# Splitting three attentions into six pairs of heads between the halves of an output projection

## The chip, the cores and the metric

The kernel runs on one core of a Trainium2 chip. The metric is the device time of one launch in microseconds (us), as the median of several runs. Engines are called by the profile's names: PE (TensorE's matmuls), PEld (its weight loads), ACT (ScalarE), DVE (VectorE), POOL (GpSimd), SP (SyncE, which issues the weight transfers).

## What is computed

A sequence of 256 tokens of width 1024 goes through two blocks of two layers each, all in float32. The change lies in the mixer of the first block's second layer:

```python
c_q, c_kv, k_r, q_mem = split(h @ mla_w_in)        # 384, 256, 64, 512 columns
q  = (rmsnorm(c_q) @ w_uq).reshape(B, S, 8, 192)   # 128 plain + 64 rotary
kv = (rmsnorm(c_kv) @ w_ukv).reshape(B, S, 8, 256) # 128 keys + 128 values
q_nope, q_rope, k_nope = each head's part, rmsnorm over the head, rotary on q_rope
o = causal softmax attention, 8 heads, 256 queries, 256 keys
o_mem = softmax attention of q_mem's 4 heads into 256 memory tokens (no mask)
x = x + concatenate([o, o_mem]) @ w_out            # 1536 x 1024
```

Before and after the mixer stands a gated feed-forward layer (1024 to 2816 and back).

## The kernel before

**Weights** come in slots of 128 x 2048 float32 (1 MB). SP loads slot after slot in a fixed order into a ring of three buffers; ACT rounds each to a high part (`act_hi`, L233) and DVE takes the remainder (`dve_lo`, L238), so a product is three fast matmuls (`pe_weight`, L242 to L244: high x high, high x low, low x high). SP reloads a buffer once its remainder is taken (`lo_ready`); ACT overwrites a high part once PE has used the slot (`slot_used`). Products that use no weight slot (norm sums, scores, transposes, values) are plain float32 matmuls, which the profile counts as two instructions each.

**Order.** Each engine has its own program, written out by hand and executed in order; semaphores join them. The mixer of this layer is `pe_mla`, `act_mla`, `dve_mla` and `pool_mla` (L1331 to L1604). Its second half has two parts.

*The up-projection* makes seven products in PSUM, `chunk(0)` to `chunk(6)`: the rotary queries, heads 0 to 3 and 4 to 7 of keys and queries, and the values of the two token tiles (5 and 6). They take turns in banks 4 to 5 and 6 to 7. Chunks 0 to 4 are copied to SBUF by DVE (`copy(i)`), squared by POOL (`pool_mla`, L1522), summed over the head by PE (`sums(i)`, L340, two matmuls of 512 columns), turned into a factor by ACT (`factor(i)`: logarithm L326, exponential L330), and scaled by DVE (`norm(i)`, L879).

*The three attentions*, numbered 1 (the four memory heads), 2 and 3 (four causal heads each), use four banks at a time, 4 to 7 for attentions 1 and 3, 0 to 3 for 2. Each goes through the same chain: scores (PE, L789); mask for 2 and 3 (DVE, L819); row maximum and its negative (DVE, L823, L826); exponential with row sums (ACT, L835); reciprocal and scaling (DVE, L842, L846); transposes (PE, L800); copy to SBUF (ACT, L851); product with the values (PE, L808, L810); split of the result into high (ACT, L309) and low part (DVE, L313), which are the inputs of the output projection. The output projection (`pe_out`) accumulates in banks 0 to 3. It has six slots of two 128-row halves: slots 0 and 1 take the memory heads, 2 and 3 attention 2, 4 and 5 attention 3. Because attention 2 also occupies banks 0 to 3, the accumulator is cleared (`pe_clear_acc`, L303) after attention 2 is split. On PE the order is

```python
scores(1); scores(2); turn(1); attend(1); turn(2); scores(3); attend(2)
clear; out 0; out 1; out 2; turn(3); out 3; attend(3); out 4; out 5
```

Of the kernel before, what the change touches and what calls it, by code (L numbers as in the profile page):

```python
# [26 lines left out]
P = 128  # L27
# [82 lines left out]
def build(nc, d_slots, d_x, d_mem, d_params, d_params2, d_consts, d_lngb, d_out):  # L110
    with ExitStack() as ctx:
# [89 lines left out]
        att_act, att_dve, att_pe = ([sem(f"att_{e}{n}") for n in range(4)] for e in ("act", "dve", "pe"))  # L201
# [558 lines left out]
        ATT_MLA = (2, 3)  # L760
        ATT_SCALE = (128 ** -0.5, 128 ** -0.5, (128 + 64) ** -0.5, (128 + 64) ** -0.5)
        att_small = sb("att_small", [P, 4, 4, 8])

        def att_rows(n):

            return [att_small[:, n, i].rearrange("p (t h) -> p t h", t=2) for i in range(4)]
# [6 lines left out]
        def att_view(n, v):  # L773
            return v[:, 0:HEADS * (384 if n in ATT_MLA else 512)].rearrange("p (h k) -> p h k", h=HEADS)

        def att_ps(n, b):
            return ps[:, b:b + 4, 0:384 if n in ATT_MLA else 512]

# [4 lines left out]
        def pe_scores(pe, n, b, products):  # L783

            for h in range(HEADS):
                for t in range(2):
                    pairs = products(h, t)
                    for i, (q, k) in enumerate(pairs):
                        last = pe.matmul(att_tile(n, att_ps(n, b), t)[:, h], q, k[:, 0:att_keys(n, t)], start=(i == 0),  # L789
                                         stop=(i == len(pairs) - 1), skip_group_check=True)  # L790
            last.then_inc(att_pe[n], 1)

        def pe_turn(pe, n, b, probs):
            out, src = att_ps(n, b), att_view(n, probs)
            pe.wait_ge(att_dve[n], AD("probs"))
            for h in range(HEADS):
                for t in range(2):
                    for m in range(att_keys(n, t) // P):
                        o = m * 256 + (t - (n in ATT_MLA and m)) * P
                        last = pe.transpose(out[:, h, o:o + P], att_tile(n, src, t)[:, h, m * P:(m + 1) * P], ident)  # L800
            last.then_inc(att_pe[n], 1)

        def pe_attend(pe, n, b, probs_t, value):

            out, src = banks(b, 2, HEADS, T), att_view(n, probs_t)
            pe.wait_ge(att_act[n], AA("copied"))
            for h in range(HEADS):
                pe.matmul(out[:, h], value(h, 0), src[:, h, 0:T], start=True, stop=False, skip_group_check=True)  # L808
                o = out[:, h, P:T] if n in ATT_MLA else out[:, h]
                last = pe.matmul(o, value(h, 1), src[:, h, T:], start=False, stop=True, skip_group_check=True)  # L810
            last.then_inc(att_pe[n], 1)

        def dve_att_max(dve, n, b, probs):
# [3 lines left out]
            if n in ATT_MLA:  # L817

                dve.tensor_tensor(att_view(n, probs), src, bcast(const("causal"), HEADS), ALU.add).then_inc(att_masked, 1)  # L819
                src = att_view(n, probs)  # L820
                dve.wait_ge(att_masked, ATT_MLA.index(n) + 1)
# [6 lines left out]
        def act_att_exp(act, n, b, probs):  # L828
# [4 lines left out]
            for h in range(HEADS):  # L833
# [5 lines left out]
        def dve_att_scale(dve, n, probs):  # L839
# [4 lines left out]
            for t in range(2):  # L844
                v = att_tile(n, att_view(n, probs), t)
                last = dve.tensor_tensor(v, v, row_rec[:, t].unsqueeze(2).to_broadcast([P, HEADS, att_keys(n, t)]), ALU.mult)  # L846
# [6 lines left out]
        def act_att_parts(act, n, b, k0, at, m):  # L853

            act.wait_ge(att_pe[n], AP_("out"))
            act_split(act, banks(b, 2, HEADS, T)[:, k0:k0 + m], in_hi[:, at:at + m])

        def dve_att_parts(dve, sp, b, k0, at, m):
            dve_split(dve, sp, banks(b, 2, HEADS, T)[:, k0:k0 + m], in_hi[:, at:at + m], in_lo[:, at:at + m])


# [134 lines left out]
        SPLIT_GLA, SPLIT_LAT, SPLIT_MLA = 3, 11, 14  # L996
        SPLIT_B2, SPLITS2 = 17, 10
# [191 lines left out]
        def dve_gla(dve):  # L1189
# [98 lines left out]
            dve_att_parts(dve, SPLIT_MEMO[0], 4, 0, 8, 2)  # L1288
            dve_att_parts(dve, SPLIT_MEMO[0] + 1, 4, 2, 10, 2)
# [19 lines left out]
        m_probs = {1: view(9728, 2048), 2: view(11776, 2048), 3: view(9728, 2048)}  # L1309
        m_probs_t = view(13824, 2048)  # L1310
# [20 lines left out]
        def pe_mla(pe):  # L1331
# [75 lines left out]
            chunk(6)  # L1407

            pe.wait_ge(mla_act, MA("v1"))
            pe_scores(pe, 1, 4, lambda h, t: [(m_qm[:, h, t * P:(t + 1) * P], mem_k[:, h])])  # L1410

            def products(g):
                def of(h, t):
                    h = 4 * g + h
# [3 lines left out]
                return of  # L1418

            def value(g):  # L1420
                return lambda h, m: m_v[:, m, (4 * g + h) * P:(4 * g + h + 1) * P]
            pe.wait_ge(mla_dve, MD("qr_turned"))
            pe.wait_ge(rms_dve, RMS_CHUNK + 3)
            pe.wait_ge(rms_act, RA("log", RMS_CHUNK + 4))
            pe_scores(pe, 2, 0, products(0))
            pe_turn(pe, 1, 4, m_probs[1])
            pe_attend(pe, 1, 4, m_probs_t, lambda h, m: mem_v[:, m, h * P:(h + 1) * P])
            pe_turn(pe, 2, 0, m_probs[2])
            pe.wait_ge(split_lo, SPLIT_MEMO[1] + 1)
            pe.wait_ge(rms_dve, RMS_CHUNK + 5)  # L1430
            pe_scores(pe, 3, 4, products(1))
            pe_attend(pe, 2, 0, m_probs_t, value(0))
            pe.wait_ge(split_lo, SPLIT_MLA + 1)
            pe_clear_acc(pe)
            for i in range(3):
                pe_out(pe, L1_OUT, i, MLA_OUT_AT)
            pe_turn(pe, 3, 4, m_probs[3])
            pe_out(pe, L1_OUT, 3, MLA_OUT_AT)
            pe_attend(pe, 3, 4, m_probs_t, value(1))
            pe.wait_ge(split_lo, SPLIT_MLA + 2)  # L1440
            pe_out(pe, L1_OUT, 4, MLA_OUT_AT)
            pe.wait_ge(split_lo, SPLIT_MLA + 3)
            pe_out(pe, L1_OUT, 5, MLA_OUT_AT)

        def act_mla(act):
# [38 lines left out]
            def value(t):  # L1484
                wait_chunk(act, 5 + t)
                act.activation(m_v[:, t], chunk_ps(5 + t), ACT.Copy).then_inc(mla_act, 1)
            act_hi(act, c + 2)
            act_hi(act, c + 3)
            act_rms_factor(act, RMS_MEMQ[1], head_sums, m_qm_factor, 128)
            act_hi(act, c + 4)  # L1490
            factor(0)
            factor(1)
            act_hi(act, c + 5)
            factor(2)
            act_hi(act, c + 6)
            factor(3)
            value(0)
            factor(4)
            value(1)
            act_att_exp(act, 1, 4, m_probs[1])  # L1500
            act_hi(act, L1_OUT + 2)
            act_att_turned(act, 1, 4, m_probs_t)
            act_att_exp(act, 2, 0, m_probs[2])
            act_att_parts(act, 1, 4, 0, 8, 4)
            act_att_turned(act, 2, 0, m_probs_t)
            act_att_parts(act, 2, 0, 0, 0, 4)
            act_att_exp(act, 3, 4, m_probs[3])
            act_hi(act, L1_OUT + 3)
            act_hi(act, L1_OUT + 4)
            act_att_turned(act, 3, 4, m_probs_t)  # L1510
            act_hi(act, L1_OUT + 5)
            act_att_parts(act, 3, 4, 0, 4, 2)
            act_att_parts(act, 3, 4, 2, 6, 2)
            act_hi(act, L1_OUT + 6)
            act_hi(act, L1_OUT + 7)

        def pool_mla(pool):
            for i, (v, _, _) in enumerate(CHUNKS):
                pool.wait_ge(mla_dve, MD(f"copy{i}"))
                if i >= 2:  # L1520
                    pool.wait_ge(rms_pe, RMS_CHUNK + i - 1)
                pool.tensor_tensor(m_sq[i % 2], v, v, ALU.mult).then_inc(mla_sq, 1)  # L1522

        def dve_mla(dve):
# [26 lines left out]
            def norm(i):  # L1551
                dve_head_norm(dve, RMS_CHUNK + i, CHUNKS[i][0], CHUNKS[i][1], m_factor[i % 2])
            dve_lo(dve, c + 2)
            copy(0)
            dve_lo(dve, c + 3)
            dve_head_norm(dve, RMS_MEMQ[1], flat(m_qm), "memq1", m_qm_factor)
            copy(1)
            dve_lo(dve, c + 4)
# [4 lines left out]
            dve_lo(dve, c + 5)  # L1563
# [7 lines left out]
            dve_lo(dve, c + 6)  # L1571
            norm(3)
            norm(4)
            dve_att_max(dve, 1, 4, m_probs[1])
            dve_att_scale(dve, 1, m_probs[1])
            dve.wait_ge(rms_dve, RMS_CHUNK + 5)
            dve_att_max(dve, 2, 0, m_probs[2])
            dve_lo(dve, L1_OUT + 2)
            dve_att_scale(dve, 2, m_probs[2])
            dve_att_parts(dve, SPLIT_MEMO[1], 4, 0, 8, 4)  # L1580
            dve_att_max(dve, 3, 4, m_probs[3])
            dve_att_parts(dve, SPLIT_MLA, 0, 0, 0, 4)
            dve_att_scale(dve, 3, m_probs[3])
            dve_lo(dve, L1_OUT + 3)
            dve_lo(dve, L1_OUT + 4)
            dve_lo(dve, L1_OUT + 5)
            dve_att_parts(dve, SPLIT_MLA + 1, 4, 0, 4, 2)
            dve_att_parts(dve, SPLIT_MLA + 2, 4, 2, 6, 2)
            dve_lo(dve, L1_OUT + 6)
# [703 lines left out]
        def _(pool):  # L2293
# [9 lines left out]
            pool_mla(pool)  # L2303
# [235 lines left out]
```

## Time and profile before

| | us |
|---|---|
| median of 3 runs (2076.99 to 2081.15) | 2080.57 |
| time of the profiled execution | 2082.32 |
| span of the profiled execution | 2080.2 |
| PE busy in the span | 2047.2 |
| DVE, ACT, POOL busy in the span | 1271.8, 999.4, 86.8 |

The span runs from the first to the last instruction of the profile. PE's busy time is the time in which at least one matmul is in the array; it says nothing of how fast the array ran, which the granted clock tells (1.00 is full speed, 0.50 half).

### The profile page before, as it was taken

The numbers are of one execution on the slowest core, as the hardware profiler recorded it, in microseconds if no ns is written. First come the engines' busy times: TensorE is split into PE (matmuls) and PEld (weight loads), VectorE is DVE, ScalarE is ACT, GpSimd is POOL, SyncE is SP. The second block draws the span as 40 slices with busy tenths as digits, with TensorE's granted clock in tenths as the row PEclk, the third lists the DMA queues.
The fourth block names the chain that finished last, engine by engine and source line by source line (L and its number), as shares of the span: only waits on it lengthen the run. The fifth ranks groups of instructions, "written<-read, shape, count | busy, mean of one in ns | idle before, by whom it ended". The sixth has DMA issues, their size and how long they took to land.

```text
span 2080.2 us, 37327 instructions
## 1 busy us (share of the span) xinstructions
PE 2047.2 (98%) x15913; PEld 1959.2 (94%) x15928; DVE 1271.8 (61%) x1141; ACT 999.4 (48%) x929; POOL 86.8 (4%) x58
## 2 busy tenths in 40 slices
PE   9999999999999999899999999999999999999998
PEld 8999998999999998589999999999998999999997
DVE  6556655755665576637555665676446674676545
ACT  5545645543454356435344663544344554544333
POOL 2000000100000001101000000100000000100000
PEclk9999999999999999999999999999999999999999
DMA  7555453455555544125554434464554544464552
GB/s 297 182 181 182 166 178 118 161 188 181 181 203 182 192 179 174 61 87 206 181 187 179 164 141 163 176 243 166 183 192 157 197 142 142 167 228 183 192 181 102
DMA packets 51217, 362.31 MB, mean 174 GB/s; under 512 B 5680, under 2 KB 6832, under 8 KB 7728
## 3 DMA queue, kind: packets, MB, share of 16 engines
q1 hardware_dynamic: 49856, 353.05, 47.4%
q0 software_dynamic: 1264, 7.80, 1.1%
q8 instruction: 81, 1.33, 0.2%
q14 instruction: 16, 0.13, 0.0%
HBM read 359.78 MB, written 1.05 MB: 173 GB/s over the span
## 4 chain that ended last, share of the span: by engine, by line
PE 92%; DVE 3%; ACT 2%; DMA 1%; issue 1%; POOL 0%; DVEq 0%; SPq 0%; ACTq 0%; POOLq 0%
PE ps L242 22%; PE ps L243 22%; PE ps L244 22%; PE ps L518 3%; PE ps L519 3%; PE ps L517 3%; PE ps L289 2%; PE ps L290 2%; PE ps L291 2%; PE ps L501 1%; PE ps L495 1%; PE ps L496 1%; DMA raw<-in_slots 1%; PE ps L789 1%; PE ps L1619 1%
## 5 line engine op out<-in xcount | busy, mean ns | idle before, releaser
L238 DVE TENSOR_TENSOR wlo<-raw,whi 128x2048 fp32r<-128x2048 f32 x325 | 758.9, 2337 | 476.4 <-ACT whi L233 475.6
L242 PE MATMUL ps<-in_hi,whi 128*128 128x256 f32 x3596 | 1016.7, 283 | 3.8 <-DVE in_lo L313 3.5
L243 PE MATMUL ps<-in_lo,whi 128*128 128x256 f32 x3596 | 1006.5, 280 | 0.0
L244 PE MATMUL ps<-in_hi,wlo 128*128 128x256 f32 x3596 | 1005.3, 280 | 0.0
L233 ACT ACTIVATE whi<-raw 128x2048 fp32r<-128x2048 f32 x325 | 619.4, 1908 | 214.8 <-PE ps L244 184.4
L242 PEld LDWEIGHTS ps<-in_hi,whi 128*128 128x128 f32 x3596 | 678.6, 189 | 12.3 <-DVE in_lo L313 4.7
L243 PEld LDWEIGHTS ps<-in_lo,whi 128*128 128x128 f32 x3596 | 678.7, 189 | 3.5 <-issue 1.7
L244 PEld LDWEIGHTS ps<-in_hi,wlo 128*128 128x128 f32 x3596 | 678.4, 189 | 0.0
L242 PE MATMUL ps<-h_hi,whi 128*128 128x256 f32 x480 | 134.5, 280 | 0.0
L243 PE MATMUL ps<-h_lo,whi 128*128 128x256 f32 x480 | 133.9, 279 | 0.0
L244 PE MATMUL ps<-h_hi,wlo 128*128 128x256 f32 x480 | 133.9, 279 | 0.0
L642 ACT ACTIVATE h_hi<-ws 128x512 fp32r<-128x512 f32 x58 | 36.7, 633 | 196.0 <-PE ps L519 99.4
L712 DVE TENSOR_TENSOR h_lo<-ws,h_hi 128x512 fp32r<-128x512 f32 x58 | 40.9, 706 | 103.1 <-ACT h_hi L642 103.1
L636 ACT ACTIVATE ws<-ws 128x512 f32<-128x512 f32 x44 | 27.8, 632 | 148.1 <-DVE ws L695 148.1
L519 PE MATMUL ps<-whi,h_lo 128*128 128x512 f32 x240 | 94.9, 396 | 0.0
L518 PE MATMUL ps<-wlo,h_hi 128*128 128x512 f32 x240 | 94.9, 396 | 0.0
L517 PE MATMUL ps<-whi,h_hi 128*128 128x512 f32 x240 | 94.9, 395 | 0.0
L289 PE MATMUL ps<-whi,in_hi 128*128 128x256 f32 x320 | 91.1, 285 | 0.0
L242 PEld LDWEIGHTS ps<-h_hi,whi 128*128 128x128 f32 x480 | 90.2, 188 | 0.4
L243 PEld LDWEIGHTS ps<-h_lo,whi 128*128 128x128 f32 x480 | 90.2, 188 | 0.1
L244 PEld LDWEIGHTS ps<-h_hi,wlo 128*128 128x128 f32 x480 | 90.2, 188 | 0.0
L290 PE MATMUL ps<-wlo,in_hi 128*128 128x256 f32 x320 | 89.9, 281 | 0.0
(295 smaller groups left out, 2162.9 us busy)
## 6 DMA issues: line engine op xcount, KB each, us to landing
raw<-in_slots SPq DMA_DIRECT2D x333, 1024.0 KB, 4.8
ws<-in_lngb POOLq DMA_DIRECT2D x4, 1024.0 KB, 5.1
ws<-in_mem_t POOLq DMA_DIRECT2D x2, 1024.0 KB, 10.1
consts<-in_consts SPq DMA_DIRECT2D x1, 1600.0 KB, 14.6
consts<-in_consts POOLq DMA_DIRECT2D x1, 1472.0 KB, 6.7
x<-in_x_t SPq DMA_DIRECT2D x1, 1024.0 KB, 7.9
y<-x SPq DMA_DIRECT2D x1, 512.0 KB, 2.6
y<-x SPq DMA_DIRECT2D x2, 256.0 KB, 2.1
```

The lines of the kernel that those rows point to most:

```text
L233: act.activation(whi[:, j], raw[:, j], ACT.Copy).then_inc(hi_ready, 1)
L238: dve.tensor_tensor(wlo[:, j], raw[:, j], whi[:, j].bitcast(F32), ALU.subtract).then_inc(lo_ready, 1)
L242: pe.matmul(out, whi[:, j, o:o + n], hi, start=start, stop=False, skip_group_check=True)
L243: pe.matmul(out, whi[:, j, o:o + n], lo, start=False, stop=False, skip_group_check=True)
L244: return pe.matmul(out, wlo[:, j, o:o + n], hi, start=False, stop=stop, skip_group_check=True)
L289: pe.matmul(o, a_hi, w_hi, start=(k == 0), stop=False)
L290: pe.matmul(o, a_hi, w_lo, start=False, stop=False)
L291: last = pe.matmul(o, a_lo, w_hi, start=False, stop=(k == DT - 1))
L517: pe.matmul(o, hi[:, kk, a], whi[:, j, w], start=(first and kk == 0), stop=False, skip_group_check=True)
L518: pe.matmul(o, hi[:, kk, a], wlo[:, j, w], start=False, stop=False, skip_group_check=True)
L519: last = pe.matmul(o, lo[:, kk, a], whi[:, j, w], start=False, stop=False, skip_group_check=True)
L712: dve.tensor_tensor(flat(lo), src, flat(hi).bitcast(F32), ALU.subtract).then_inc(ffn_hl, 1)
```

## The change

The three attentions become six of two heads: 1 and 2 are the memory heads, 3 to 6 the causal heads. Each uses two banks, odd ones 6 and 7, even ones 4 and 5 (`pair_bank`), and its own pair of SBUF buffers by parity (`pair_probs`). The accumulator's banks 0 to 3 belong to the projection from then on; it is cleared right after `chunk(6)`. A slot of the projection is worked off in halves (`pe_out_part`: 24 matmuls for each 128-row half), and the halves stand between an attention's transposes, the next one's scores, and its product with the values. ACT and DVE get the same steps in an order that fits. The squares of chunks 0 to 4 move from POOL to ACT (`square`); `pool_mla` is gone. DVE's remainders of four weight slots come one or two steps later. The number and the shapes of PE's matmuls and transposes stay the same. The core of the diff (the helpers take `ATT_HEADS[n]` in place of `HEADS` throughout):

```diff
-        ATT_MLA = (2, 3)
+        ATT_MLA = (3, 4, 5, 6)
+        ATT_HEADS = (HEADS, 2, 2, 2, 2, 2, 2)
+        def pe_out_part(pe, c, i, at, kk, ms):
+            j = (c + i) % RING
+            if kk == 0:
+                pe.wait_ge(lo_ready, c + i + 1)
+            a_hi, a_lo = in_hi[:, at[2 * i + kk]], in_lo[:, at[2 * i + kk]]
+            for m in ms:
+                last = pe_weight(pe, acc[:, m], j, kk * D + m * P, a_hi, a_lo, False, False)
+            return last
...
+        PAIR_AT = (8, 10, 0, 2, 4, 6)
+        def pair_bank(n):
+            return 6 if n % 2 else 4
+        def pair_probs(n):
+            return m_probs[(n - 1) % 2], m_probs_t[(n - 1) % 2]
...
+            def scores(n):
+                if n >= 3:
+                    pe.wait_ge(split_lo, SPLIT_MEMO[1] + n - 2)
...
+            def out(i, kk, ms=range(DT)):
+                if kk == 0:
+                    pe.wait_ge(split_lo, SPLIT_MEMO[1] + i + 1)
+                return pe_out_part(pe, L1_OUT, i, MLA_OUT_AT, kk, ms)
+            pe.wait_ge(mla_act, MA("v0"))
+            scores(1)
+            chunk(6)
+            pe.wait_ge(rms_act, RA("log", RMS_CHUNK + 4))
+            pe_clear_acc(pe)
+            pe.wait_ge(mla_act, MA("v1"))
+            scores(2)
+            turn(1)
+            attend(1)
             pe.wait_ge(mla_dve, MD("qr_turned"))
             pe.wait_ge(rms_dve, RMS_CHUNK + 3)
...
+            scores(3)
+            out(0, 0)
+            turn(2)
+            out(0, 1, range(4))
+            attend(2)
+            out(0, 1, range(4, DT)).then_inc(slot_used, 1)
+            for n in range(3, 7):
+                turn(n)
+                if n == 4:
+                    pe.wait_ge(rms_dve, RMS_CHUNK + 5)
+                if n < 6:
+                    scores(n + 1)
+                out(n - 2, 0)
+                attend(n)
+                out(n - 2, 1).then_inc(slot_used, 1)
+            out(5, 0)
+            out(5, 1).then_inc(slot_used, 1)
...
         def act_mla(act):
...
+            def square(i):
+                act.wait_ge(mla_dve, MD(f"copy{i}"))
+                if i >= 2:
+                    act.wait_ge(rms_pe, RMS_CHUNK + i - 1)
+                act.activation(m_sq[i % 2], CHUNKS[i][0], ACT.Square).then_inc(mla_sq, 1)
...
             act_hi(act, c + 2)
+            act_rms_factor(act, RMS_MEMQ[1], head_sums, m_qm_factor, 128)
+            square(0)
             act_hi(act, c + 3)
+            square(1)
+            factor(0)
             act_hi(act, c + 4)
             factor(1)
+            square(2)
+            square(3)
+            factor(2)
             act_hi(act, c + 5)
+            square(4)
             factor(3)
             value(0)
             factor(4)
+            exp(1)
             value(1)
+            act_hi(act, L1_OUT + 1)
+            turned(1)
+            parts(1)
+            exp(2)
             act_hi(act, L1_OUT + 2)
+            exp(3)
+            turned(2)
+            parts(2)
+            for n in range(3, 7):
+                turned(n)
+                if n < 6:
+                    exp(n + 1)
+                parts(n)
+                act_hi(act, L1_OUT + n)
             act_hi(act, L1_OUT + 7)
...
         def dve_mla(dve):
...
             norm(3)
+            att_max(1)
             norm(4)
+            scale(1)
+            att_max(2)
+            dve_lo(dve, L1_OUT + 1)
+            parts(1)
+            att_max(3)
+            scale(2)
+            dve_lo(dve, L1_OUT + 2)
+            scale(3)
+            parts(2)
+            for n in range(3, 7):
+                if n < 6:
+                    att_max(n + 1)
+                parts(n)
+                if n < 6:
+                    scale(n + 1)
+                dve_lo(dve, L1_OUT + n)
             dve_lo(dve, L1_OUT + 7)
...
-            pool_mla(pool)
```

## Rows read from the trace of the kernel before

**Rows 1.** The page: span and busy time of each engine.
```profile
span 2080.2 us, 37327 instructions
...
PE 2047.2 (98%) x15913; PEld 1959.2 (94%) x15928; DVE 1271.8 (61%) x1141; ACT 999.4 (48%) x929; POOL 86.8 (4%) x58
```

**Rows 2.** Busy time by stage, all engines.
```profile
core 0: us, PE busy (x) PEld busy (x) DVE busy (x) ACT busy (x) POOL busy (x), PEclk, DMA share, GB/s
...
600.00:780.00 180.00, 180.00 (x1539) 179.83 (x1538) 110.65 (x96) 81.08 (x66) 3.89 (x3) 1.00 0.51 185
780.00:936.00 156.00, 139.91 (x897) 117.74 (x897) 86.51 (x69) 76.32 (x104) 13.64 (x6) 0.97 0.30 108
```

**Rows 3.** TensorE's waits, 740 to 980 us: total, times, longest.
```profile
PE ps L340 <- POOL ws L1522: 5.0, 2, 3.0
PE ps L800 <- DVE ws L846: 2.8, 2, 1.9
PE ps L303 <- DVE in_lo L313: 2.6, 1, 2.6
PE ps L808 <- ACT ws L851: 2.0, 1, 2.0
PE ps L242 <- DVE in_lo L313: 1.9, 2, 1.4
PE ps L789 <- ACT ws L1486: 1.1, 1, 1.1
```

**Rows 4.** Clock in stretches of 4 us of that stage (columns as Rows 2).
```profile
828.00:832.00 4.00, 4.00 (x20) 3.38 (x19) 1.29 (x2) 2.17 (x2) 1.89 (x1) 0.60 0.26 107
848.00:852.00 4.00, 3.80 (x6) 1.71 (x7) 1.23 (x1) 0.02 (x1) 0.15 (x1) 0.57 0.56 233
...
868.00:872.00 4.00, 3.42 (x16) 3.15 (x16) 3.97 (x4) 0.00 (x0) 0.00 (x0) 0.60 0.00 0
...
892.00:896.00 4.00, 1.40 (x10) 1.05 (x11) 2.43 (x3) 3.75 (x14) 0.00 (x0) 1.00 0.00 0
```

**Rows 5.** The chain that ended last in the stage: start us, us, what.
```profile
855.79 3.74 PE ps L789 x16
...
868.59 3.57 PE ps L800 x16
...
874.05 3.51 ACT ws L835 x16
...
881.23 8.16 PE ps L789 x32
...
934.88 0.43 DVE x L748
```

**Rows 6.** ScalarE in order of time.
```profile
809.79 1.05 ACT L322 ACTIVATE ws<-ws 128x1024 f32<-128x1024 f32 x1
```

**Rows 7.** Weight loads in order of time, start of the stage.
```profile
809.68 0.19 PEld L242 LDWEIGHTS ps<-in_hi,whi 128*128 128x128 f32 x1 [0.91 <-DVE in_lo L313]
...
813.88 0.30 PEld L340 LDWEIGHTS ps<-ws,consts 128*128 128x128 f32 x2
```

**Rows 8.** Groups by shape, 811 to 935 us.
```profile
L1522 POOL TENSOR_TENSOR ws<-ws 128x1024 f32<-128x1024 f32 x5 | 13.4, 2685 | 74.8 <-DVE ws L1549 74.8
...
L819 DVE TENSOR_TENSOR ws<-ps,consts 128x1536 f32<-128x1536 f32 x2 | 3.5, 1754 | 8.6 <-PE ps L789 8.6
...
L851 ACT ACTIVATE ws<-ps 128x1536 f32<-128x1536 f32 x2 | 2.9, 1452 | 7.3 <-PE ps L800 7.3
...
L846 DVE TENSOR_TENSOR ws<-ws,att_small 128x512 f32<-128x512 f32 x2 | 1.4, 692 | 0.1
L823 DVE TENSOR_REDUCE att_small<-ws 128x4 f32<-128x512 f32 x2 | 1.4, 686 | 0.1
L313 DVE TENSOR_TENSOR in_lo<-ps,in_hi 128x512 fp32r<-128x512 f32 x2 | 1.3, 686 | 3.3 <-ACT in_hi L309 3.3
...
L309 ACT ACTIVATE in_hi<-ps 128x512 fp32r<-128x512 f32 x2 | 1.1, 594 | 5.0 <-PE ps L810 5.0
```

More of the change, by code:

```diff
@@ L200, in build @@
         gla_act, gla_dve, gla_pe, gla_norm = sem("gla_act"), sem("gla_dve"), sem("gla_pe"), sem("gla_norm")
-        att_act, att_dve, att_pe = ([sem(f"att_{e}{n}") for n in range(4)] for e in ("act", "dve", "pe"))
+        att_act, att_dve, att_pe = ([sem(f"att_{e}{n}") for n in range(7)] for e in ("act", "dve", "pe"))
         att_masked, mla_sq = sem("att_masked"), sem("mla_sq")
@@ L759, in build @@
         AP_, AD, AA = steps("scores", "turned", "out"), steps("max", "neg", "recip", "probs"), steps("exp", "copied")
-        ATT_MLA = (2, 3)
-        ATT_SCALE = (128 ** -0.5, 128 ** -0.5, (128 + 64) ** -0.5, (128 + 64) ** -0.5)
-        att_small = sb("att_small", [P, 4, 4, 8])
+        ATT_MLA = (3, 4, 5, 6)
+        ATT_SCALE = (128 ** -0.5,) * 3 + ((128 + 64) ** -0.5,) * 4
+        ATT_HEADS = (HEADS, 2, 2, 2, 2, 2, 2)
+        att_small = sb("att_small", [P, 7, 4, 8])
         def att_rows(n):
-            return [att_small[:, n, i].rearrange("p (t h) -> p t h", t=2) for i in range(4)]
+            return [att_small[:, n, i, 0:2 * ATT_HEADS[n]].rearrange("p (t h) -> p t h", t=2) for i in range(4)]
         def att_keys(n, t):
@@ L783, in pe_scores @@
         def pe_scores(pe, n, b, products):
-            for h in range(HEADS):
+            for h in range(ATT_HEADS[n]):
                 for t in range(2):
@@ L795, in pe_turn @@
             pe.wait_ge(att_dve[n], AD("probs"))
-            for h in range(HEADS):
+            for h in range(ATT_HEADS[n]):
                 for t in range(2):
@@ L803, in pe_attend @@
         def pe_attend(pe, n, b, probs_t, value):
-            out, src = banks(b, 2, HEADS, T), att_view(n, probs_t)
+            out, src = banks(b, ATT_HEADS[n] // 2, ATT_HEADS[n], T), att_view(n, probs_t)
             pe.wait_ge(att_act[n], AA("copied"))
-            for h in range(HEADS):
+            for h in range(ATT_HEADS[n]):
                 pe.matmul(out[:, h], value(h, 0), src[:, h, 0:T], start=True, stop=False, skip_group_check=True)
@@ L817, in dve_att_max @@
             if n in ATT_MLA:
-                dve.tensor_tensor(att_view(n, probs), src, bcast(const("causal"), HEADS), ALU.add).then_inc(att_masked, 1)
+                dve.tensor_tensor(att_view(n, probs), src, bcast(const("causal"), ATT_HEADS[n]), ALU.add).then_inc(att_masked, 1)
                 src = att_view(n, probs)
@@ L832, in act_att_exp @@
             act.wait_ge(att_dve[n], AD("neg"))
-            for h in range(HEADS):
+            for h in range(ATT_HEADS[n]):
                 for t in range(2):
@@ L845, in dve_att_scale @@
                 v = att_tile(n, att_view(n, probs), t)
-                last = dve.tensor_tensor(v, v, row_rec[:, t].unsqueeze(2).to_broadcast([P, HEADS, att_keys(n, t)]), ALU.mult)
+                last = dve.tensor_tensor(v, v, row_rec[:, t].unsqueeze(2).to_broadcast([P, ATT_HEADS[n], att_keys(n, t)]), ALU.mult)
             last.then_inc(att_dve[n], 1)
@@ L1406, in pe_mla @@
             sums(4)
[L1407 to L1412, printed above, removed]
+            def scores(n):
+                if n >= 3:
+                    pe.wait_ge(split_lo, SPLIT_MEMO[1] + n - 2)
                 def of(h, t):
-                    h = 4 * g + h
+                    if n < 3:
+                        h = 2 * (n - 1) + h
+                        return [(m_qm[:, h, t * P:(t + 1) * P], mem_k[:, h])]
+                    h = 2 * (n - 3) + h
                     r = slice(64 * (h % 2), 64 * (h % 2) + 64)
@@ L1417, in of, with turn, attend, value @@
                             (m_qr[r, h // 2, t * P:(t + 1) * P], m_kr[r, :])]
-                return of
-            def value(g):
-                return lambda h, m: m_v[:, m, (4 * g + h) * P:(4 * g + h + 1) * P]
+                pe_scores(pe, n, pair_bank(n), of)
+            def turn(n):
+                pe_turn(pe, n, pair_bank(n), pair_probs(n)[0])
+            def attend(n):
+                def value(h, m):
+                    if n < 3:
+                        h = 2 * (n - 1) + h
+                        return mem_v[:, m, h * P:(h + 1) * P]
+                    h = 2 * (n - 3) + h
+                    return m_v[:, m, h * P:(h + 1) * P]
+                pe_attend(pe, n, pair_bank(n), pair_probs(n)[1], value)
@@ L1423, in pe_mla @@
             pe.wait_ge(rms_dve, RMS_CHUNK + 3)
[L1424 to L1443, printed above, removed]
+            scores(3)
@@ L1486, in value, with exp, turned, parts @@
                 act.activation(m_v[:, t], chunk_ps(5 + t), ACT.Copy).then_inc(mla_act, 1)
+            def square(i):
[3 more added lines that the diff above has]
+                act.activation(m_sq[i % 2], CHUNKS[i][0], ACT.Square).then_inc(mla_sq, 1)
+            def exp(n):
+                act_att_exp(act, n, pair_bank(n), pair_probs(n)[0])
+            def turned(n):
+                act_att_turned(act, n, pair_bank(n), pair_probs(n)[1])
+            def parts(n):
+                act_att_parts(act, n, pair_bank(n), 0, PAIR_AT[n - 1], 2)
             act_hi(act, c + 2)
+            act_rms_factor(act, RMS_MEMQ[1], head_sums, m_qm_factor, 128)
+            square(0)
             act_hi(act, c + 3)
-            act_rms_factor(act, RMS_MEMQ[1], head_sums, m_qm_factor, 128)
+            square(1)
+            factor(0)
             act_hi(act, c + 4)
-            factor(0)
             factor(1)
+            square(2)
+            square(3)
+            factor(2)
             act_hi(act, c + 5)
-            factor(2)
-            act_hi(act, c + 6)
+            square(4)
             factor(3)
@@ L1552, in norm, with att_max, scale, parts @@
                 dve_head_norm(dve, RMS_CHUNK + i, CHUNKS[i][0], CHUNKS[i][1], m_factor[i % 2])
+            def att_max(n):
+                dve_att_max(dve, n, pair_bank(n), pair_probs(n)[0])
+            def scale(n):
+                dve_att_scale(dve, n, pair_probs(n)[0])
+            def parts(n):
+                dve_att_parts(dve, n, SPLIT_MEMO[1] + n - 1, pair_bank(n), 0, PAIR_AT[n - 1], 2)
             dve_lo(dve, c + 2)
             copy(0)
-            dve_lo(dve, c + 3)
             dve_head_norm(dve, RMS_MEMQ[1], flat(m_qm), "memq1", m_qm_factor)
             copy(1)
-            dve_lo(dve, c + 4)
+            dve_lo(dve, c + 3)
             norm(0)
@@ L1562, in dve_mla @@
             copy(3)
-            dve_lo(dve, c + 5)
+            dve_lo(dve, c + 4)
             dve.wait_ge(mla_turn, MT("qr"))
```

58 lines of the change are left out of this document (11 added, 47 removed).

## Prediction

> **What bounds the kernel now.** I read the page first: PE is busy for 2047.2 of 2080.2 us and no other engine for more than 61% [rows 1], so only time in which PE waits, or runs at a lower clock, can be won. Next, busy time by stage. In a feed-forward stage PE is busy for 180.00 of 180 us; in the stage that holds the changed mixer for 139.91 of 156 us, at a mean clock of 0.97 [rows 2]. That is where the kernel has slack, and the change touches nothing else. The part it rewrites begins with the first matmul of `chunk(0)` at 809.7 us [rows 7] and ends when DVE adds the finished projection to x at 934.9 us [rows 5]: 125.2 us. The waits of PE name what it loses there: 5.0 us for POOL's squares, 2.8 for scaled probabilities (L846) before transposes, 2.6 and 1.9 for low parts of an attention's result, 2.0 for the copy of transposed probabilities, 1.1 for the value copy; 15.4 us together [rows 3]. About 0.5 of it is the wait just ahead of `chunk(0)` (the weight load there was free for 0.91 us) [rows 7], so I count 14.9 us of waiting in the part. Then the clock: it was at the lower of its levels, 1.2 in place of 2.4 GHz, for most of three stretches of 4 us, with means of 0.60, 0.57 and 0.60 [rows 4]. Each costs 4 x 0.4 or so, 1.65 us, and the three 4.9. What is left, 125.2 - 14.9 - 4.9 = 105.4 us, is PE's work at full speed.
>
> **What the change leaves alone.** PE's matmuls stay: same number, same shapes, only their order differs, so 105.4 us stay. PE gets more waits, some two dozen, but a wait whose event is long past shows no gap in the trace, so I charge nothing; a tenth of a microsecond each would be 2.4, which goes into the range. SP's order of slots is the same. Four remainders (slots 3 and 4 of the up-projection, 0 and 1 of the output) come behind one more DVE step of 1.3 us or an attention step; each is still done 5 us or more before PE needs it, by the walk below, and the loads that wait for them start as much later, with as much to spare. Slots 2 to 5 of the projection are prepared once a round, a whole round ahead.
>
> **Squares.** A square costs 2.7 us on POOL on average (13.4 for five) [rows 8], on ACT 1.05 (the same size, L322) [rows 6]. That takes 1.65 us out of copy, square, sum. The 5.0 us of PE's waits for POOL came to 2.0 and 3.0; the second (square 4) goes altogether, since `copy(4)` also comes earlier, with no clock loss ahead of it, and PE has `chunk(5)` to do. ACT executes in order, so square 2 stands behind `factor(1)`, which waits for `sums(1)`, and square 3 for `copy(3)`. Walking the three queues forward with these durations I get one wait of 0.6 us, for square 2 ahead of `sums(2)`. The five squares add 5.2 us to ACT, which was busy for 76.3 of 156 us [rows 2]; its waits cover them.
>
> **Attentions 1 and 2 (memory).** Halved steps cost: transposed copy (L851, 1.45 for four causal heads) 0.8, with memory's wider tile 1.0; exponential (3.51 for four heads [rows 5]) 1.85 with the last row sum; mask 0.9 from 1.75; reductions 1.3 (2 x 0.69, causal 1.1); scaling 1.4 (causal 1.1); split 0.6 and 0.69 [rows 8]; scores of a memory pair 1.9 and a causal pair 4.1 from 3.74 and 8.16 [rows 5]. The walk from there:
> - scores(1) needs only the first value copy and runs before `chunk(6)`, so the 1.1 us wait goes. But ACT does exp(1) before the second value copy, and exp(1) waits for maximum and negative. `chunk(6)` (12 matmuls of 512 columns at twice 0.117, 2.8 us) and the clear (four of 512, 0.9) don't quite cover it: scores(2) waits 1.0.
> - turn(1) finds its probabilities ready. attend(1) waits for the copy with nothing placed between: 1.2 (2.0 before).
> - scores(3) takes banks 6 and 7 over from attention 1, so it waits until both parts of attention 1 are split: 0.6 + 0.69 and hand-overs. New, 1.6.
> - Half a slot (24 matmuls at 0.117, since 36 took 4.2 us [rows 7], 2.8 us) then covers part of DVE's mask, maxima, negative and scale(2), which stand in this order behind scores(3): turn(2) waits 1.2.
> - attend(2) is covered by the quarter slot ahead of it.
>
> **The rounds.** From n = 3 on a round is turn, scores(n+1), half slot, attend, half slot: 0.65 + 4.1 + 2.8 + 1.4 + 2.8 = 11.75 us of PE. (The transposes: 3.57 us for 16 instructions at the lower clock [rows 5] makes 0.67 for six at the higher; the product with the values: four instructions of 256 columns at 0.23, from scores(1), and four of 128 at half of it.) Behind scores(n+1) mask, maxima, negative and exponential take 0.9 + 1.1 + 0.2 + 1.85 = 4.05, against half slot and attend, 4.2. Behind attend come high part 0.6, low part 0.69, reciprocal 0.2 and scaling 1.1, 2.7 with overlaps, against the last half slot's 2.8. So PE doesn't wait, by a hair. The splits that cost 2.6 and 1.4 of waiting before [rows 3] now have a half slot behind them, the last one too.
>
> **Sum.** New waits 0.6 + 1.0 + 1.2 + 1.6 + 1.2 = 5.6 for 14.9: 9.3 us less. The clock: before, its falls stood behind waits for POOL (2.0 and 3.0) and behind the 0.9 ahead of turn(1), yet a wait of 2.6 us at 892 left it at 1.00 [rows 3, 4]; the trace gives no fixed length from which it falls. No new wait is above 1.6, but four stand within 20 us. Bounds: no fall (4.9 gained) to three (nothing); I take one, near the row at 868, so 4.9 - 1.65 = 3.25 gained. That makes 12.5; I round to 13, since POOL no longer runs beside DVE in this part. By the profiled execution the span would be 2067.2. Its own time, 2082.32, is 1.75 above the median, so I take the difference off the median: 2080.57 - 13 = 2067.5.
>
> The clock is also where a page speaks against the change. The Trainium skill, "TensorE: Matmul & The Clock Gate", section "A second HAM failure mode: psum-queue depth-cycling", says that a PE which idles briefly again and again between groups of matmuls while it cycles through PSUM banks sees its clock go down and up. By that rule the lower clock would come in most rounds, as in the third case below; the trace agrees only for the stretch at 868, not for 892.
>
> **Rivals.** Bounds first: without any fall and with two waits fewer the gain is 14.9 - 4 + 4.9 = 16 us (2064.5).
> 1. *The forecast*, 2064 to 2070: 0.60.
> 2. *The handoffs become the bound.* The margins of the rounds are 0.1 us. For it speaks that DVE and ACT run parts, scaling and slot work in one queue; against it that both are busy for under 60% of the part [rows 2]. One microsecond late in each of four rounds, or ACT late with each square (5 x 1), gives 4 to 5 back: 2072, range 2070 to 2074. 0.17.
> 3. *The clock falls three to five times* through the short steps, 3.3 to 6.6 us more than forecast: 2071 to 2074. For it, the fall behind a wait of 0.9; against it, that each round has 5.6 us of the dense matmuls that ran at 1.00 throughout. 0.10.
> 4. *Nothing comes of it*: the first feed-forward slots are late, so the gain is given back at the next stage. They are prepared behind attention 6 and wait for slots 3 and 4 to be used; I see their remainders done 1 us before the projection ends. 2077 to 2084: 0.05.
> 5. *Slower*: the clock stays at 1.2 GHz through the rounds. From 850 us on PE has about 65 us of work at full speed, and each microsecond of it at the half clock costs one more; from 12.5 us so spent the gain is gone. With two rounds at the half clock (23 us) the time is 2091. Turn(1) took 3.57 us for 16 instructions at the lower clock [rows 5], so it does reach transposes; but before no low stretch lasted beyond 4 us [rows 4]. 0.08.
>
> **How the numbers follow.** The likeliest case gives 2067.5, by itself 2064 to 2070. The runs of one kernel differ by up to 4 us, so its lower end becomes 2062, and cases 2 and 3 take the range to 2075; that leaves out cases 4 and 5 and the tails. A change of 0.2% (4.2 us) is about what a measurement of this kernel can tell. Faster: 0.60 + 0.17 + 0.10 = 0.87; same 0.06; slower 0.07; case 4 falls within 0.2%, case 5 all but one in eight on the slow side.
>
> **What would show it.** POOL has nothing between the mix squares and the end of the mixer. No wait of PE for L340's input above 1 us. Scores(3) waits 1.6 us for L313. From the third round of the projection on PE's busy time is full, and the part takes about 112 us. Wrong would be: waits of PE for DVE L846 in each round, PE's clock below 0.8 in several stretches after 850 us, or a wait of PE for a weight slot (L238) at the start of the next feed-forward.

## The result and the profile after

The changed kernel takes 2066.9 us (median of four runs, 2065.5 to 2068.5) where the kernel before, on the same chip, takes 2080.9 (2077.0 to 2081.4). The ratio is 0.9938, 95% interval 0.9923 to 0.9952, so it is faster by 14.0 us or 0.6%. The forecast was 2067.5.

TensorE's waits in the window of [rows 3]:

```profile
PE ps L790 <- DVE in_lo L313: 1.5, 1, 1.5
PE ps L809 <- ACT ws L852: 1.1, 1, 1.1
PE ps L790 <- ACT ws L1526: 0.8, 1, 0.8
PE ps L273 <- ACT in_hi L603: 0.6, 1, 0.6
PE ps L242 <- DVE in_lo L313: 0.5, 1, 0.5
PE ps L340 <- ACT ws L1531: 0.4, 1, 0.4
```

L790, L809 and L340 are scores, product with the values, and norm sums. Without the 0.6 and 0.5 us, which lie outside the part, PE waits 3.8 us for 14.9 before: 0.4 ahead of `sums(2)`, 0.8 ahead of scores(2), 1.1 ahead of attend(1), 1.5 ahead of scores(3). Those are the waits of the walk (0.6, 1.0, 1.2, 1.6), each a tenth or two shorter; the fifth, 1.2 ahead of turn(2), is missing. The next view, busy time in stretches, tells why (columns as in [rows 2], the clock is the third value from the end):

```profile
852.00:856.00 4.00, 2.60 (x14) 1.80 (x12) 3.42 (x4) 1.27 (x2) 0.00 (x0) 1.00 0.00 0
856.00:860.00 4.00, 2.78 (x11) 1.69 (x11) 0.69 (x1) 3.97 (x10) 0.00 (x0) 0.93 0.74 262
860.00:864.00 4.00, 4.00 (x11) 2.48 (x12) 0.96 (x2) 0.00 (x0) 0.00 (x0) 0.50 0.00 0
864.00:868.00 4.00, 4.00 (x28) 4.00 (x28) 3.93 (x7) 1.86 (x8) 0.00 (x0) 0.72 0.00 0
868.00:872.00 4.00, 4.00 (x30) 3.79 (x29) 1.93 (x4) 1.49 (x2) 0.00 (x0) 1.00 0.46 152
```

The clock fell right after the three waits, once, and stayed at 1.2 GHz for some 7 us (4 x (0.07 + 0.50 + 0.28) = 3.4 us lost, at half speed 6.8 us long). The chain shows what it cost (start us, us, what):

```profile
855.75 0.61 ACT in_hi L309
856.38 0.70 DVE in_lo L313
...
857.22 5.75 PE ps L790 x16
...
867.49 0.87 PE ps L801 x8
...
872.90 0.65 PE ps L801 x6
873.55 3.98 PE ps L790 x16
...
884.66 0.66 PE ps L801 x6
885.31 3.98 PE ps L790 x16
...
896.41 0.66 PE ps L801 x6
...
908.16 0.66 PE ps L801 x6
...
921.37 0.44 DVE x L748
```

Scores(3) took 5.75 us, scores(4) and (5), the same work, 3.98. The half slot behind scores(3) ran slowly too, long enough for DVE to have turn(2)'s probabilities ready at 867.49. So part of what the lower clock cost was time that PE would otherwise have waited. From 872.90 on the rounds start every 11.75 us (872.90, 884.66, 896.41, 908.16) with no wait, the length that the forecast added up. POOL has no instruction in the part, as forecast. The part begins at 809.5 us and ends at 921.4, 111.8 us long (125.2 before, about 112 forecast).

The span fell by 16.5 us, 3.1 more than the part. The remainder, from the end of the part to the end of the span, is the same program: 1145.3 us before, 1142.3 after. Over all the profiles of this study it lies between 1140.5 and 1145.3, with low-clock stretches near 1220 and 1700 us of the execution now longer, now shorter. They explain the spread. Adding up length times one minus clock over all stretches of 4 us of the remainder gives 8.2 us lost before and 4.4 after, and what is left of the remainder without its loss is between 1136.9 and 1137.9 us in each of the 13 profiles. So the 3 us that the span fell beyond the part are clock, not work.

The same split can be made for every execution, since each has its span and mean clock on record. Span times clock, an estimate of the time at full clock throughout (good to 1 us, because the clock is given to three decimals), has a median of 2064.7 us over 34 executions of the kernel before (2062.5 to 2066.2) and of 2053.4 over 14 of the changed one (2052.0 to 2054.6). About 11 us of the gain are waits and order, and the 3 to 5 that are left are a clock that is low for less time, in the part and behind it.

### The profile page after: what moved, and what is told of

Read it like the earlier page. It is cut to its first block, busy times and chain, and to the rows that moved or that the text cites. A ratio compares the mean times of both kernels' runs of the same rounds, so it can differ in the third digit from the quotient of the medians.

```text
span 2063.7 us, 37372 instructions
## 1 busy us (share of the span) xinstructions
PE 2042.7 (99%) x15928; PEld 1956.7 (95%) x15928; DVE 1267.6 (61%) x1163; ACT 1004.7 (49%) x939; POOL 73.3 (4%) x53
## 4 chain that ended last, share of the span: by engine, by line
PE 94%; DVE 3%; ACT 2%; DMA 1%; issue 1%; DVEq 0%; SPq 0%; ACTq 0%
PE ps L242 23%; PE ps L244 22%; PE ps L243 22%; PE ps L518 3%; PE ps L519 3%; PE ps L517 3%; PE ps L291 2%; PE ps L289 2%; PE ps L290 2%; PE ps L790 1%; PE ps L501 1%; PE ps L495 1%; PE ps L496 1%; DMA raw<-in_slots 1%; ACT whi L233 1%; PE ps L340 1%
## 5 line engine op out<-in xcount | busy, mean ns | idle before, releaser
L238 DVE TENSOR_TENSOR wlo<-raw,whi 128x2048 fp32r<-128x2048 f32 x325 | 755.6, 2327 | 456.5 <-ACT whi L233 455.7
```

Of the source, the lines that this page charges most:

```text
L238: dve.tensor_tensor(wlo[:, j], raw[:, j], whi[:, j].bitcast(F32), ALU.subtract).then_inc(lo_ready, 1)
```

## The experiments

All comparisons are with runs of the kernel before on the same chip. "Part" is the stretch from the first matmul of `chunk(0)` to the first addition to x, in the profiled execution. Rows with the same time before ran on the same chip.

| kernel | median us (runs) | before | ratio, 95% interval | part us |
|---|---|---|---|---|
| changed | 2066.9 (4) | 2080.9 | 0.9938, 0.9923 to 0.9952 | 111.8 |
| squares alone | 2074.3 (9) | 2080.3 | 0.9973, 0.9964 to 0.9983 | 117.0 |
| split alone | 2067.6 (5) | 2080.3 | 0.9942, 0.9929 to 0.9956 | 114.4 |
| filled waits | 2064.4 (5) | 2080.3 | 0.9920, 0.9907 to 0.9934 | 109.8 |
| no interleaving | 2099.4 (4) | 2080.3 | 1.0090, 1.0074 to 1.0105 | 146.8 |
| changed, second | 2065.4 (5) | 2079.6 | 0.9931, 0.9917 to 0.9945 | 111.8 |
| slot work first | 2071.3 (5) | 2079.6 | 0.9960, 0.9946 to 0.9973 | 117.8 |
| no interleaving, filled | 2085.3 (7) | 2079.6 | 1.0027, 1.0016 to 1.0038 | 131.9 |
| filled and shifted | 2064.6 (5) | 2079.6 | 0.9918, 0.9903 to 0.9933 | 109.4 |
| changed, third | 2063.6 (5) | 2079.4 | 0.9927, 0.9913 to 0.9941 | 113.4 |
| split alone, second | 2066.6 (5) | 2079.4 | 0.9942, 0.9928 to 0.9955 | 114.4 |
| filled and shifted, second | 2064.6 (5) | 2079.4 | 0.9927, 0.9913 to 0.9940 | 109.3 |

### The squares alone

```diff
 # kernel before, act_mla
             act_rms_factor(act, RMS_MEMQ[1], head_sums, m_qm_factor, 128)
+            square(0)
             act_hi(act, c + 4)
+            square(1)
             factor(0)
             factor(1)
+            square(2)
+            square(3)
             act_hi(act, c + 5)
             factor(2)
             act_hi(act, c + 6)
+            square(4)
             factor(3)
...
-            pool_mla(pool)
```

> The kernel before with one part of the change: the five squares on ACT instead of POOL, three attentions and the projection as before. Theory A (the squares matter through TensorE's clock and the DVE instructions that POOL stretched): the 5.0 us of waits for POOL shrink to about 3, since walking the queues forward with the rows' durations leaves PE's waits at 13.5 us for 14.2, but the two low-clock stretches behind the POOL waits (828 and 848 us) go and DVE's remainders next to a square fall from 3.3 to 4.0 us back to 2.3: 3 to 5 us faster, near 2077. Rival B (only the length of the waits counts): under 1 us, no measurable change, and the low-clock stretches stay.

6.0 us faster, a little more than the 3 to 5 of theory A. TensorE's waits, and DVE's remainders (L238: shortest, median and longest ns) in this kernel and in the one before:

```profile
PE ps L800 <- DVE ws L846: 2.8, 2, 1.9
PE ps L303 <- DVE in_lo L313: 2.6, 1, 2.6
...
PE ps L340 <- ACT ws L1491: 1.5, 2, 1.0
```

```profile
L238 DVE TENSOR_TENSOR wlo<-raw,whi x5: 2279/2293/2293, 811.5 to 840.8; 128x2048 fp32r<-128x2048 f32 x5
```

```profile
L238 DVE TENSOR_TENSOR wlo<-raw,whi x5: 2276/2293/4033, 812.7 to 844.1; 128x2048 fp32r<-128x2048 f32 x5
```

The squares now cost 1.5 us of waiting for 5.0, where the walk had left 3; the waits of the attentions are as before. The longest remainder fell from 4.03 to 2.29 us, so the slow ones were those beside POOL. In the profiled execution the clock stayed at 1.00 through the whole part and the part was 8.2 us shorter: 3.5 of waits, the rest the low clock. The fall at 868 us is gone too, though the wait of 0.9 ahead of turn(1) is still there, so that wait alone doesn't make it. This profile is of the fastest of nine executions, which spread from 2069 to 2079 us, wider than any other kernel here. The spread goes with the clock: the fastest has a mean clock of 0.998 and the two slowest 0.992, and 0.006 of the span is 12 us. Which stretches it fell in is known for the profiled one only.

### The split alone

```diff
 # changed kernel
-            square(0)            # and 1 to 4, in act_mla
...
+            pool_mla(pool)       # as before
```

> The changed kernel with the squares back on POOL. Theory A: walking forward, PE's waits in the part grow from 5.5 to 7.9 us, and one or two low-clock stretches of 1.7 us come back with the waits for POOL: 3 to 6 us slower than the changed kernel, 2070 to 2073. If the two parts of the change are independent, its gain and that of the squares alone add up to the 14 us of the whole. Rival B: the squares are hidden, 2067 to 2068.

> The changed kernel with the squares on POOL, on the same chip as the changed kernel. The medians so far, from two chips, lie 0.7 us apart, but in the profiled executions the part took 4 us longer with POOL. Theory A (the squares bring something only where PE's waits ahead of the sums are not made up for later; the 3.1 us of waits for POOL are on PE's path): 3 to 4 us slower than the changed kernel. Rival B (what POOL costs is given back, since a low-clock stretch falls there instead of at scores(3)): within 1 us.

12.8 us faster than before both times. The first time, 2067.6 us lies in the range of rival B and below that of theory A, but the changed kernel had run on another chip. Beside the changed kernel on the same chip it is 3.0 us slower (2066.6 and 2063.6, the ranges of the runs don't meet: 2066.3 to 2067.7 and 2063.5 to 2065.7), at the lower end of theory A. The profile of the second time:

```profile
PE ps L340 <- POOL ws L1575: 3.1, 2, 2.4
PE ps L790 <- DVE in_lo L313: 1.5, 1, 1.5
...
PE ps L801 <- DVE ws L847: 0.7, 1, 0.7
```

```profile
840.00:844.00 4.00, 1.62 (x5) 0.67 (x4) 4.00 (x2) 1.16 (x2) 2.94 (x1) 0.88 0.35 104
844.00:848.00 4.00, 4.00 (x11) 2.29 (x10) 0.02 (x1) 1.20 (x2) 0.00 (x0) 0.69 0.37 158
...
860.00:864.00 4.00, 3.66 (x15) 2.21 (x16) 0.19 (x1) 3.09 (x7) 0.00 (x0) 1.00 0.61 246
```

The wait for POOL is 3.1 us in all, the low clock comes behind it (844) and not at scores(3) (860), and the wait of 0.7 for DVE at turn(2) is back. The first profile shows the same, with the low clock from 846 to 850. The three waits ahead of scores(2), attend(1) and scores(3) are 0.8, 1.1 and 1.5 us as in the changed kernel, and yet the clock is 1.00 behind them in both profiles. So the two parts don't add up: 6.0 and 12.8 us alone, 14.0 to 15.8 together. Rival B's mechanism is seen, but it gives back only a part.

### No half slots between the steps

```diff
 # changed kernel, pe_mla (act_hi and dve_lo of slots 3 to 7 follow the last attention too)
             scores(3)
-            out(0, 0)
             turn(2)
-            out(0, 1, range(4))
             attend(2)
...
                 turn(n)
                 scores(n + 1)
-                out(n - 2, 0)
                 attend(n)
-                out(n - 2, 1).then_inc(slot_used, 1)
+            for i in range(6):
+                out(i, 0)
+                out(i, 1).then_inc(slot_used, 1)
```

> The changed kernel with pairs of heads, their banks and the squares on ACT, but with no half slot between the steps: all six slots of the projection follow the last attention, and their weight preparation follows it too. Theory A (the half slots are what hides the chains): walking forward, PE's waits grow from 5.5 to 28 us, and low-clock stretches with them, 2 to 5 of them at 1.7 us: 26 to 31 us slower than the changed kernel, 2093 to 2098, so slower than before. Rival B (finer attentions alone bring the gain, by overlapping with one another): within 5 us of the changed kernel, 2067 to 2072.

19 us slower than before and 32.5 slower than the changed kernel, which had run on another chip (33.0 when each is taken against the kernel before on its own chip). That is a little beyond theory A's 26 to 31. Waits, and the clock in four of the stretches:

```profile
PE ps L801 <- DVE ws L847: 16.2, 4, 5.0
PE ps L809 <- ACT ws L852: 3.1, 3, 1.1
PE ps L790 <- DVE in_lo L313: 2.3, 2, 1.5
```

```profile
884.00:888.00 4.00, 2.09 (x9) 1.87 (x10) 1.80 (x4) 0.52 (x1) 0.00 (x0) 0.50 0.02 4
888.00:892.00 4.00, 4.00 (x10) 2.25 (x10) 0.00 (x0) 0.29 (x1) 0.00 (x0) 0.50 0.00 0
...
904.00:908.00 4.00, 4.00 (x9) 2.25 (x10) 0.00 (x0) 0.00 (x0) 0.00 (x0) 0.50 0.00 0
908.00:912.00 4.00, 4.00 (x10) 2.43 (x10) 1.97 (x4) 0.00 (x0) 0.00 (x0) 0.50 0.00 0
```

The pairs of heads by themselves gain nothing. Each attention waits 3.7 to 5.0 us for its scaled probabilities, and behind such waits the scores ran at 1.2 GHz from one wait to the next (7.40 us for scores(4) and scores(5), 4.14 in the changed kernel). This is the mechanism of the fifth rival of the prediction; it needs waits that the changed kernel no longer has. To separate the waits from the clock, matmuls of zeros were put ahead of them:

```diff
+            def fill(n):
+                for _ in range(n):
+                    pe.matmul(ps[:, 0, :], zeros[:, 0:P], zeros[:, :], start=False, stop=False, skip_group_check=True)
...
             for n in range(3, 7):
+                if n > 3:
+                    fill(24)
                 turn(n)
```

> The kernel without interleaving (all six slots of the projection behind the last attention) with matmuls of zeros (0.21 us each) put ahead of PE's waits, as many as fit into each: 3, 4, 6 at the first three, 18, 5, 3 around attention 2, 24 ahead of the transposes of attentions 4 to 6, 4 ahead of the last product with the values. PE has just as long to wait, but its array is busy meanwhile. Theory A (the 32.5 us that the lack of interleaving costs are 22.5 us of waits by the walk and some 10 us of the lower clock): the clock stays at 1.00 in the part and the kernel is 7 to 10 us faster than without the fill, 2089 to 2092. Rival B (all of it is the waits themselves, since DVE and ACT set the pace of the chain and PE's speed doesn't matter there): within 3 us of 2099.

14 us faster than without the fill (13.4 against the kernel before on each chip), more than the 7 to 10 that theory A expected. The clock stayed at 1.00 throughout the part, which is 14.9 us shorter. So of the 33 us that it costs to leave the half slots out, 13 to 14 are the clock, and 20 (2085.3 and 2065.4 on one chip) are time in which the array has nothing of its own to do.

### The waits that are left

> The changed kernel with 13 matmuls of zeros (512 columns, bf16, 0.21 us each, they add zero to the accumulator) put into PE's three waits ahead of scores(2), attend(1) and scores(3): 3, 4 and 6 of them. They fit into the waits of 0.8, 1.1 and 1.5 us. Theory A (the waits made the clock fall at 859 us, and the fall costs 3.4 us of which 1.2 is hidden by a wait at turn(2)): the clock stays at 1.00, scores(3) takes 4.0 us instead of 5.75, a wait of about 1.2 us shows at turn(2), net 2 us faster than the changed kernel, 2065. Rival B (the short matmuls of scores(3) themselves lower the clock): the fall stays, no change or 0.5 us slower.

```diff
+            fill(3)
             pe.wait_ge(mla_act, MA("v1"))
             scores(2)
             turn(1)
+            fill(4)
             attend(1)
+            fill(6)
```

PE in order of time (start us, us):

```profile
855.27 0.70 PE L809 MATMUL ps<-ws 128*128 128x256 f32 x2 [0.25 <-ACT ws L852]
...
858.77 4.22 PE L790 MATMUL ps<-ws 128*128 128x128 f32 x16 [0.21 <-DVE in_lo L313]
...
866.69 1.09 PE L801 MATMUL ps<-consts,ws 128*128 128x128 f32 x8 [0.68 <-DVE ws L847]
```

The clock stayed at 1.00 in the part, scores(3) took 4.22 us, and the wait at turn(2) appeared, 0.7 us for the 1.2 expected; the time is 2064.4 for 2065. The short matmuls of scores(3) don't lower the clock by themselves. The fall at 860 needs the idle time of the waits: it stands in all five profiles with these waits open and the squares on ACT, and in none of the four with the waits filled. It isn't enough, since both profiles of the split alone have the same three waits and no fall there. The next kernel also moves six matmuls ahead of turn(2).

```diff
             out(0, 0)
+            out(0, 1, range(2))
             turn(2)
-            out(0, 1, range(4))
+            out(0, 1, range(2, 5))
             attend(2)
-            out(0, 1, range(4, DT)).then_inc(slot_used, 1)
+            out(0, 1, range(5, DT)).then_inc(slot_used, 1)
```

> The changed kernel with the 13 matmuls of zeros in its three first waits, and with 6 of the 12 matmuls of the quarter slot that follows turn(2) moved ahead of it (0.7 us), where the filled kernel showed a wait of 0.7 us; 9 matmuls (1.05 us) remain to cover the copy of 1.02 us ahead of attend(2). Expected 0.5 to 0.7 us faster than the filled kernel, 2063.7, and 3 us faster than the changed kernel; a rival says that the shift only moves the wait to attend(2), no gain.

> The kernel with filled waits and the shifted quarter slot, on the same chip as the changed kernel, which the two calls before left undecided (0.9 us, intervals overlapping). The part itself is 2.4 us shorter in the trace, so 2 to 3 us faster than the changed kernel if the clock's falls elsewhere (1220, 1696 us) come alike; a rival says that those are set by chance and hide it.

The part is 109.4 us for 111.8, and the waits left in it are 0.4, 0.3 and 0.2 us. But the time doesn't follow. Beside the changed kernel on the same chip it is 0.9 us faster on one chip and 1.0 slower on the other, where 3 and 2 to 3 faster were expected. In all three profiles of filled kernels the clock fell more near 1220 us than in the changed kernel's, for instance in the last, and below it the changed kernel's first:

```profile
1216.00:1220.00 4.00, 4.00 (x11) 1.79 (x10) 4.00 (x7) 1.50 (x4) 0.00 (x0) 0.81 0.29 78
1220.00:1224.00 4.00, 4.00 (x21) 4.00 (x20) 2.40 (x8) 1.55 (x2) 0.00 (x0) 0.50 0.45 188
1224.00:1228.00 4.00, 4.00 (x31) 4.00 (x31) 0.00 (x0) 3.99 (x3) 0.00 (x0) 0.84 0.00 0
```

```profile
1220.00:1224.00 4.00, 4.00 (x19) 3.24 (x18) 4.00 (x11) 0.00 (x0) 0.00 (x0) 0.66 0.75 266
1224.00:1228.00 4.00, 4.00 (x33) 4.00 (x33) 0.37 (x1) 3.57 (x3) 0.00 (x0) 0.92 0.00 0
```

The remainder of the span is 1143.5 to 1145.1 us in them and 1140.5 to 1142.3 in the three of the changed kernel. The difference is the clock alone: it costs 6.3 to 8.0 us there in the filled kernels and 2.8 to 4.6 in the changed one. Over the whole span the loss is 8.0 to 11.4 us with the waits filled and 9.5 to 9.7 without, so what the fill saves in the part is lost again behind it. Single executions do escape: the filled and shifted kernel had two at 2059.9 and 2060.3 us with a mean clock of 0.998, below any of the changed kernel (2063.3 at best, 0.996). Why the clock falls more there stays open: the instructions are the same, and PE has no wait between 1190 and 1230 us. The low stretch begins in or behind eight matmuls whose weights have 4 rows (L1856 in the changed kernel, 3.7 us in all), and PE is busy throughout. The changed kernel in its other executions:

> The changed kernel once more, on the same chip as the three kernels beside it, to compare them directly: 2065 to 2069.

> The changed kernel, once more beside the two kernels of this call: 2065 to 2069.

It took 2065.4 and, below the expected range, 2063.6 us, 14.2 and 15.8 less than before.

### How thin the cover of the rounds is

```diff
 # changed kernel, act_mla, in each round
+                act_hi(act, L1_OUT + n)
                 parts(n)
-                act_hi(act, L1_OUT + n)
```

> The changed kernel with ACT's high part of a weight slot (1.9 us) ahead of the high parts of an attention in each of the four rounds, instead of behind. Theory A (the rounds' chain behind attend is covered by a hair, 0.1 us): the transposes of rounds 4, 5 and 6 each wait about 1.8 us for DVE, and the last slot 0.4; walking forward, PE's waits grow from 5.5 to 10.7 us, 5 us slower than the changed kernel, 2072, and more if the clock falls too. Rival B (there is slack of 1 us or more in the rounds): under 2.5 us slower.

5.9 us slower than the changed kernel beside it (2071.3 and 2065.4). Its waits:

```profile
PE ps L801 <- DVE ws L847: 3.8, 3, 1.3
PE ps L790 <- DVE in_lo L313: 1.5, 1, 1.5
PE ps L809 <- ACT ws L852: 1.1, 1, 1.1
```

An item of 1.8 us put ahead of the splits makes each of three transposes wait 1.3. The splits themselves come only 1.5 us later, because ACT starts the item while the product with the values still runs (in the first round they start 1.93 us behind the start of that product's last instruction, in the changed kernel 0.42), so the cover exceeds the chain by 0.2 to 0.3 us. The waits are 3.8 us; another 2 come from a longer low-clock stretch at scores(3), whose length differed between executions of the changed kernel as well (its third profile: part 113.4 us). From 872 us on the clock was 1.00 in spite of the three waits.

## Why the prediction was right

- **The bound and the part.** The gain that the change itself makes lies in the part: 13.4 us in the first profile, forecast 13. Of it 11.1 are waits (forecast 9.3), 1.7 the clock (forecast 3.25), and 0.6 isn't traced to a term. What the time shows beyond the part is, by the profiles, clock in the remainder, which the forecast left as it was. That the three gains of 14.0, 14.2 and 15.8 us come as near to 13 as they do is in part luck.
- **Squares.** The waits of 3.0 and 2.0 us are gone, and the new one ahead of `sums(2)` is 0.4 (forecast 0.6). On top of the split the squares are worth 3.0 us of the time, side by side on one chip, and 1.0 to 2.6 of the part (114.4 for 113.4 and 111.8); without the split they are worth 6.
- **New waits.** Four of five came within 0.2 us of the walk, the wait at scores(3), which is the price of banks 6 and 7 being shared by odd attentions, among them. The fifth, at turn(2), didn't come because of the clock; in the three profiles with the clock at 1.00 there and the order of the change (the split alone twice, the filled waits) it came, as 0.7 us for the 1.2 of the walk.
- **The rounds.** No wait, period 11.75 us as added up. The margin behind attend was 0.2 to 0.3 us, near the 0.1 of the walk.
- **The clock.** One fall was taken, at 1.65 us; one came, of twice that cost (3.4 us by the stretches above, 5.1 in the third profile), and hid the wait at turn(2). So two mis-sized terms nearly cancel: 3.4 for 1.65, and 0 for 1.2. Two stretches, at 860 and 864, have a clock below 0.8, which comes close to one of the signs that the prediction gave for being wrong. The size was to be seen before: the prediction read the low stretches of this stage only, none beyond 4 us, while behind it the same trace has two of this size, one of them here.

```profile
1232.00:1236.00 4.00, 4.00 (x12) 1.98 (x11) 4.00 (x8) 1.07 (x3) 0.00 (x0) 0.75 0.35 125
1236.00:1240.00 4.00, 4.00 (x20) 4.00 (x20) 1.97 (x7) 1.98 (x2) 0.00 (x0) 0.50 0.34 141
1240.00:1244.00 4.00, 4.00 (x33) 4.00 (x32) 0.34 (x1) 3.97 (x4) 0.00 (x0) 0.90 0.00 0
```

- **The cause of the fall.** That it needs the idle time of the waits is shown by the filled kernels; what else it needs is open, as the split alone shows. The page's rule, the Trainium skill, "TensorE: Matmul & The Clock Gate", section "A second HAM failure mode: psum-queue depth-cycling", named as a case against the change: the traces agree for the three waits of the changed kernel and for the kernel without interleaving. In the rounds of the changed kernel PE doesn't idle, so nothing there tests it. With slot work first it idles 1.3 us ahead of three transposes, 13 us apart, and the clock stayed at 1.00.
- **The rivals.** Handoffs as the bound: not seen, but 1.8 us more of ACT's work per round is enough. More falls: one fall only, but in two of the four profiles of the changed kernel and of slot work first it cost 5.1 us, as much as three. Slower through the clock: not seen, but real in the kernel without half slots, where it is 13 to 14 us.

## What to carry to other kernels

Splitting a dependent chain finer gains nothing by itself; it gains when independent dense work is cut so that a piece stands behind each link, and then the order of each engine's queue decides. To size such a change, walk all the queues forward with durations from the trace and compare each link with the piece that covers it; four of five waits came out within 0.2 us of it, the fifth 0.5 too long. Short waits in a row cost more than their length where the clock falls behind them. Filling them with matmuls of zeros gave 14 us where they were many and long, and nothing certain where three short ones were left. When two kernels differ by a few microseconds, compare span times mean clock too: it tells work and waits from the clock's falls.

## What the runs showed of the hardware

- Waits of 0.8, 1.1 and 1.5 us within 8 us were followed by 7 to 10 us at 1.2 GHz in four profiles and 14 in that without half slots, and by none in both profiles of the split alone, where the clock had last been low some 14 us before scores(3). Before the change a single wait of 2.6 us left the clock at 1.00 [rows 3, 4]. Matmuls of zeros in the three waits kept it at 1.00 in all four profiles that had them.
- The clock also falls with no wait at all: near 1220 us (1232 before) in 12 of 13 profiles, in or behind eight matmuls with 4 rows of weights.
- The same instructions lose more or less to it from one execution to the next: 2.8 to 8.2 us behind the part, and between 328 and 336 us 1.7 in ten profiles, 3.4 in one and nothing in two.
- A DVE subtraction (128 x 2048) that took 2.29 us alone took 4.03 and 3.34 beside a POOL multiplication (128 x 1024), which itself took 3.87 us at times and 1.90 at others. In each of the four times that they met before the change, the one that had begun first kept its time and the other was the longer: POOL 1.90 and DVE 4.03 at 816 us, POOL 1.90 and DVE 3.34 at 834, DVE 2.28 and POOL 3.87 at 822 and at 844.
